# Halving the columns that the block-merge matmuls of the delta-rule solve stream

## The reference, cut to what matters

```python
L = jnp.tril(jnp.einsum('bhncd,bhnjd->bhncj', k_beta, k) * decay, -1)
T = lax.linalg.triangular_solve(eye + L, jnp.broadcast_to(eye, L.shape),
                                left_side=True, lower=True, unit_diagonal=True)
...
v_new = u_c - jnp.einsum('bhcd,bhdv->bhcv', w_c, state)
...
state = state * jnp.exp(g_last)[..., None, None] + jnp.einsum('bhcd,bhcv->bhdv', k_dec, v_new)
```

## Time and profile before

| | |
|---|---|
| time before, median of 3 | 3610.3 us (3603.45 to 3616.13) |
| profiled execution, its own time | 3603.45 us |
| its span in the trace | 3601.6 us |
| mean granted clock of TensorE | 0.949 of full |
| TensorE matmul busy | 3104.5 us (86%) |
| VectorE busy | 2166.9 us (60%) |
| scans in the trace | 2410.1 to 2646.9 us and 2846.5 to 3083.5 us |

### The profile page before, as it was taken

The page is one execution under the profiler, slowest core; times in us unless marked ns, Lnnn a source line. Parts: engine busy times, 40 slices in busy tenths (PEclk is TensorE's granted clock), DMA queues, the critical chain, the costliest instruction groups (busy, mean ns, idle before and its releaser), DMA issues. The chain is left out here.

```text
span 3601.6 us, 43654 instructions
## 1 busy us (share of the span) xinstructions
PE 3104.5 (86%) x15729; PEld 2506.3 (70%) x15729; DVE 2166.9 (60%) x4125; ACT 1375.0 (38%) x2733; POOL 1144.8 (32%) x1255
## 2 busy tenths in 40 slices
PE   5899878778998797798998998977879688799988
PEld 3578745555786456587887886767767578688777
DVE  6799787566997875776773014457856478201333
ACT  1366355213663552334662212344423443221221
POOL 2246321231462212622004242134432344424330
PEclk9999999989999999899999999989989899899999
DMA  6323411441234114510002113113231232412331
GB/s 213 118 77 94 130 49 57 157 139 61 77 94 132 44 56 159 181 42 7 1 1 91 50 62 116 43 33 92 66 107 41 50 94 52 158 48 94 132 102 47
DMA packets 227145, 303.10 MB, mean 84 GB/s; under 512 B 40911, under 2 KB 142031, under 8 KB 224753
## 3 DMA queue, kind: packets, MB, share of 16 engines
q1 hardware_dynamic: 215410, 279.33, 25.5%
q10 hardware_dynamic: 11520, 20.98, 1.6%
HBM read 241.91 MB, written 58.33 MB: 83 GB/s over the span
## 5 line engine op out<-in xcount | busy, mean ns | idle before, releaser
L816 PE MATMUL psum<-qs,hT 128*128 128x512 f32 x1344 | 308.5, 391 | 8.4 <-POOL qs L903 8.0
L2575 PE MATMUL psum<-hTs,cws 128*128 128x512 f32 x1152 | 281.9, 406 | 34.9 <-POOL hTs L2822 31.1
L816 PEld LDWEIGHTS psum<-qs,hT 128*128 128x128 f32 x1344 | 252.7, 189 | 64.2 <-POOL qs L903 5.7
L2575 PEld LDWEIGHTS psum<-hTs,cws 128*128 128x128 f32 x1152 | 224.5, 197 | 83.6 <-POOL hTs L2822 32.0
L2297 PE MATMUL psum<-bhsn,bringn 128*128 128x512 f32 x1152 | 264.3, 391 | 14.0 <-POOL bringn L2353 13.1
L2297 PE MATMUL psum<-bhsa,bringa 128*128 128x512 f32 x1152 | 263.9, 392 | 9.5 <-POOL bringa L2353 9.5
L2297 PEld LDWEIGHTS psum<-bhsn,bringn 128*128 128x128 f32 x1152 | 217.4, 189 | 60.8 <-issue 13.5
L2297 PEld LDWEIGHTS psum<-bhsa,bringa 128*128 128x128 f32 x1152 | 217.9, 189 | 55.5 <-issue 9.9
L1574 PE MATMUL psum<-w_out,oys 128*128 128x512 f32 x768 | 179.2, 395 | 32.9 <-DVE w_out L1657 28.5
L1574 PEld LDWEIGHTS psum<-w_out,oys 128*128 128x128 f32 x768 | 145.4, 190 | 67.6 <-DVE w_out L1657 30.1
L983 DVE TENSOR_SCALAR_CACHE_REDUCE junk<-score,cand 128x384 uint8<-128x384 f32 x248 | 186.8, 810 | 2.2
(11 more groups left out here) (491 smaller groups left out, 7037.9 us busy)
## 6 DMA issues: line engine op xcount, KB each, us to landing
stg<-in_w_in SPq DMA_DIRECT2D x96, 256.0 KB, 2.7
score<-in_w_ada SPq DMA_DIRECT2D x32, 512.0 KB, 3.9
pj<-ptmp ACTq DMA_DIRECT2D x64, 256.0 KB, 2.2
dlb<-blocks SPq DMA_DIRECT2D x32, 512.0 KB
dlb<-in_w_in SPq DMA_DIRECT2D x24, 512.0 KB, 4.0
wa<-in_w_ada SPq DMA_DIRECT2D x8, 1024.0 KB, 8.4
oyf<-yTd SPq DMA_DIRECT2D x16, 512.0 KB, 6.3
ostg<-in_w_out SPq DMA_DIRECT2D x16, 512.0 KB, 5.6
```

What stands on the lines that cost most here:

```text
L816: mm = pe.matmul(bank(m), lhs, rhs, start=(kc == 0 and x == 0), stop=(kc == KC - 1 and x == 2))
L2575: mm = pe.matmul(ps[:, u % 4, :], ws[c % 2][:, a, kc, :], hs[:, b, kc, half * HALF:(half + 1) * HALF], start=(kc == 0 and x == 0), stop=(k ...
```

## The change

`left` streams the columns of `T` that `low` selects, and writes the same columns of the bank; `right` streams and writes those that `high` selects. The number of products and their weights stay. GpSimd no longer clears `T` at the start of a scan, and VectorE's first `turn_first` no longer waits for that clearing. `X` is still cleared, and `keep_x` still waits for it.

```diff
                 for h in range(HG):
-                    mm = pe.matmul(lbank(r)[:, h, :], NLT[st % 3][r][:, h, :], T[r][:, h, :], start=True, stop=True)
+                    mm = pe.matmul(low(lbank(r), r, s)[:, h], NLT[st % 3][r][:, h, :], low(T[r], r, s)[:, h],
+                                   start=True, stop=True)
                 mm.then_inc(s_Xp, 1)
...
                 for h in range(HG):
-                    mm = pe.matmul(lbank(r)[:, h, :], X[r][:, h, :], TT[st % 3][r][:, h, :], start=True, stop=True)
+                    mm = pe.matmul(high(lbank(r), r, s)[:, h], X[r][:, h, :], high(TT[st % 3][r], r, s)[:, h],
+                                   start=True, stop=True)
                 mm.then_inc(s_Y, 1)
...
             for r in range(2):
-                pool.memset(T[r][:, :, :], 0.0)
                 ins = pool.memset(X[r][:, :, :], 0.0)
             ins.then_inc(s_X0, 1)
...
-                if st == 0 and r == 0:
-                    dve.wait_ge(s_X0, 1)
                 wide, other = (TT[st % 3][0], T[0]) if r == 0 else (T[1], TT[st % 3][1])
```

## The result

The changed kernel takes 3630.4 us (median of 4 executions, 3627.96 to 3630.89), the kernel before 3611.5 us (median of 4, one more than the three of its first measurement; 3603.45 to 3616.13). The ratio is 1.0053, with a 95% interval of 1.0035 to 1.0073: slower by half a per cent, 19.0 us. The profile after is of a fifth execution, 3636.3 us, longer than those four; the one before is of the shortest of its kernel. So the two profiles lie further apart than the medians.

The account below looks back on a forecast made before the run. Neither TensorE nor VectorE fills a scan; TensorE is the path from 2519.32 in the step read. Clock 12.8 + 3.0 + 1.4 = 17.2, tail −0.5: +16.7 on the median 3610.3 gives 3627 us, range 3607 to 3643 (8 in 10).

Parts of the forecast that it names:

- Pace, no change: Entries of `left` and `right`: weight reload sets about 112 ns each, so 64 columns save 0 over 1024 changed entries.
- the pace follows the columns: Rival: 64-column entries run faster, saving some 14 us, mostly in `left` of level 1; 3596 us; chance 0.05.
- tail: Last entry of a batch hands over up to 56 ns sooner; ten places at 0.05 us, −0.5 us.
- The clearing, nothing: Scan start: two clears of `T` leave GpSimd, but VectorE waits for a DMA of `dlb`, so 0.
- Slow writes, rejected: Rival: PSUM writes in runs with gaps are slow; 3650 us if a column is four times as dear; chance 0.06.
- The clock, the deciding term: Fewer streamed columns around TensorE's idle times make the granted clock fall to half more often; +17.2 us; chance 0.70.
- steps 2 to 5: Clock falls around the idle time before `left` of level 1: 6 of 8 passes at 2.4 us, +12.8 us net.
- Rival 1: The gate counts something else, such as weight load, and nothing moves; time 3610, delta −0.5; chance 0.17.
- steps 6 and 7: Clock falls after 2.17 us of idleness, at `left` of level 0: 3 of 4 passes, 1.0 each, +3.0 us.
- start of a scan: The clock rose during a `left` batch as the second scan began, and no longer will; +1.4 us.

Follow-up runs that it names:

- e9: The changed kernel with one-column products added in TensorE's idle times, in place of e5's wide ones; 3624.0 us, ratio 1.0049 to the kernel before.
- e1: The kernel before with only the clearing of T and VectorE's first wait taken out, all products 128 columns; 3607.3 us, ratio 0.9999.
- e4: The kernel before with `left` and `right` still at 128 columns, but reordered into runs of 16 or 32 with gaps; 3605.9 us, ratio 1.0006.
- e6: The changed kernel with 64 neighbouring columns instead of the selected ones, without gaps, output wrong; 3625.6 us, ratio 1.0053 to the kernel before.
- e5: The changed kernel with unread 128x512 products added in TensorE's idle times, 12 a scan; 3608.5 us, ratio 0.9997 to the kernel before.
- e10: The changed kernel run again unaltered, on the chip of e9; 3630.3 us, ratio 1.0067 to the kernel before.
- e2: The kernel before with only level 0 streaming 64 columns, level 1 still 128; 3620.8 us, ratio 1.0025.
- e11: The kernel of e2 (only level 0 at 64 columns) executed once more, on another chip; 3626.5 us.

## Why the prediction was right, and where its sizes were off

**Pace, no change: right.** The profile of the changed kernel has 16 entries of 64 columns in 1.90 us, (1.90 − 0.22) / 15 = 112 ns each; the 0.22 is the shortest entry in the row of `right`:

```profile
L3119 PE MATMUL psum<-dtt,dx x512: 221/275/421, 2436.7 to 3090.4; 128*128 128x64 f32 x171
```

The one-column entries at line 2644 and those of e9 say the same. So the rival "the pace follows the columns" is out, and with it any gain: all that halving the columns could save is the last entry's tail, 0.05 us a batch. That term, −0.5 us, is too small to be seen in any run.

**The clearing, nothing: right** (e1, 0.9999).

**Slow writes, rejected: right** (e4, 1.0006, and the equal times of e6 and the change).

**The clock, the deciding term: right in mechanism, and shown.** In steps 2 to 5 the wide filling takes the loss away and the narrow one doesn't (e5, e9); and the falls begin where the prediction put them, 0.4 us after `left` of level 1 starts in step 2 and 2.0 us after it in step 3 (2498.3 against 2497.87, 2529.0 against 2526.99). Rival 1, that the gate counts the time for which an entry holds TensorE, or its weight loads, is refuted by these steps of e9, where both were there in full. The mean clock of the scans is 0.86 and 0.87 where 0.89 was forecast, and in the profile after a step of 2 to 5 with a fall lasts 27.7 to 29.2 us where 28 to 29.5 was said.

**The sizes.** The two scans of the profiled execution became 25.7 us longer (493.85 − 468.19); the prediction had +16.7. By its own terms:

| term | forecast | profile after | mean of the change and e10, less that of before, e1 and e4 |
|---|---|---|---|
| steps 2 to 5 | +12.8 (6 of 8 falls) | +16.9 (8 of 8) | +13.6 |
| steps 6 and 7 | +3.0 (3 of 4, 1.0 each) | +8.3 (4 of 4) | +6.2 |
| start of a scan | +1.4 | +0.4 | −0.8 |
| tail | −0.5 | not seen | not seen |

Against the profile after, steps 2 to 5 were undercounted by two falls. The price of one was well sized: (16.9 + 1.6) / 8 = 2.3 us, against 2.4. Half of the falls were indeed twice as long.

The term that was mis-sized is steps 6 and 7. I took 1.0 us for a pass because VectorE's queue hides a part. It hides little. The start of step 6 in the changed kernel, timeline of TensorE, the place of the earlier trace rows:

```profile
2600.59 3.62 PE L3112 MATMUL psum<-dti,dnlt 128*128 128x64 f32 x16 [2.17 <-DVE dti L3472]
```

`left` takes 3.62 us, and the clock is at half for 6.8 us behind 2600.7. Step 6 was 25.60 us long and had been 23.02: 2.6 us, and 2.5 in the second scan. The fall in step 7 adds 1.6 us to the way to the scan's last product (37.00 us against 35.42).

The start came out smaller. Its terms change sign from one scan to the other: steps 0 and 1 together are 0.8 us shorter in the first and 0.8 us longer in the second. e1, which leaves the columns alone, shows a first step of 25.2 us too where before had 27.0. So this part moves from execution to execution whatever the columns are, and a single pair of profiles can't size it.

The median came near the forecast, +19.0 us where +16.7 was said, though the one profile showed +25.7. The profile of e10 has 7 falls instead of 8, and its scans are 19.95 us longer than before. If the three kernels with 128 columns (before, e1, e4: 468.2, 473.6, 474.1) are averaged, and the two with all 64 (the change, e10: 493.9, 488.1), the scans differ by 491.0 − 472.0 = 19.0 us, which is the difference of the medians. The last column of the table splits these 19.0 us. The forecast's base rate of 1 in 8 was low (6 of 24 over these three), its 6 in 8 too (15 of 16); the errors stand on the same side and mostly cancel. Steps 6 and 7 were put at half of what they cost, and the start was put at 1.4 us that didn't come; these two cancel in part as well. That the sum landed within 3 us of the medians is partly luck.

What remains of the profiled execution's +32.8 us lies outside the change: 5.45 us before the first scan begins (2415.56 against 2410.11), 0.9 us between the scans, 0.8 us behind them. Nothing before the first scan is touched, and the start of the scans in the other profiles lies anywhere from 2405.8 to 2416.5 us.

**Left open.** Why some passes fall and others don't with the same program. e2 and e11 are one kernel, with 0 and 6 falls. No run controlled that. And why steps 6 and 7 hold no fall in e9, with one-column entries in their idle time.

## What to carry to other kernels

Where the reload of its weights sets the pace of a matmul, as it did here at 112 ns an entry, streaming fewer columns saves nothing, and it can cost the clock: look beside short idle times for products that you are about to make narrower. "Busy" in the profile isn't what held the clock here (e9, steps 2 to 5); a test is to put wide products without a reader into the idle time and see whether the time comes back. And before a rate of falls is taken from a profile, count it in several executions, since one kernel had none in one and six in the next.

## What the runs showed of the hardware that was not expected

- A TensorE that was busy for 3.46 of 3.50 us with 32 entries of one and 64 columns had its clock halved in the stretch behind (e9); with 4 of 512 columns in the same place it kept 1.00 (e5).
- Falls recur in step with each other. In the changed kernel they begin at 2529.0, 2556.3 and 2583.6 us, 27.3 us apart, while the steps last 27.74 and 27.79; a fall makes a step longer, and a stretch of that length brings the same place of the next step to nearly the same moment after a fall. That this is why they recur was not tested.
- Reads and writes of fp32 in runs of 16 and 32 columns with gaps cost nothing beside the contiguous form: 1.95 us for 16 entries both ways (e4).
